# One more PSUM bank for a head's second level in the HGRN2 recurrence, and a new order on TensorE and VectorE at the change of heads

## The reference

```
bc = cumsum(log f)                                # within a chunk, per key feature
inter = einsum('bhtk,bhkv->bhtv', q * exp(b), state)
att   = einsum('bhtk,bhtsk,bhsk->bhts', q, exp(b_t - b_s), k)   # s <= t
o     = inter + einsum('bhts,bhsv->bhtv', att, v)
new_state = exp(b_last) * state + einsum('bhsk,bhsv->bhkv', k * exp(b_last - b), v)
```

## Time and profile before

| | us |
|---|---|
| median of 3 runs | 2068.59 |
| lowest and highest | 2065.93, 2070.22 |
| the profiled execution | 2072.03 |
| its span | 2070.4 |
| mean granted TensorE clock | 0.98 |
| TensorE busy | 1965.7 (95% of the span) |
| VectorE, ScalarE, GpSimd busy | 1573.7, 1342.5, 671.2 |
| the recurrence, from the first level's matmul (348.5 us) to the last output's (455.3 us) | about 107 |

### The profile page before, as it was taken

One profiled execution on the slowest core, in us unless ns is written; L12 is line 12 of the kernel. 1 busy time (PEld: TensorE's weight loads), 2 busy tenths in 40 slices (PEclk: granted clock), 3 DMA queues, 4 the chain that ended last, 5 costly groups with the idle time before them and its releaser, 6 DMA issues.

```text
span 2070.4 us, 39543 instructions
## 1 busy us (share of the span) xinstructions
PE 1965.7 (95%) x11106; PEld 1682.3 (81%) x11107; DVE 1573.7 (76%) x2202; ACT 1342.5 (65%) x1943; POOL 671.2 (32%) x758
## 2 busy tenths in 40 slices
PE   7999998879988999999999999999999999999995
PEld 6888877767776888889788897978897888979884
DVE  5334356865678788989888898889898888988886
ACT  5231156753436586877768677788777687777865
POOL 2200001321234242623425243344244252433423
PEclk9999999989978999999999999999999999999998
DMA  5322121113347898989899898999899998989987
GB/s 190 76 82 102 56 88 32 41 44 116 123 161 284 282 310 292 348 274 360 286 317 327 280 366 274 336 313 370 278 357 291 312 328 277 371 274 333 316 287 247
DMA packets 267759, 507.33 MB, mean 245 GB/s; under 512 B 39148, under 2 KB 44268, under 8 KB 267320
## 3 DMA queue, kind: packets, MB, share of 16 engines
q1 hardware_dynamic: 244042, 453.98, 63.8%
q0 software_dynamic: 23664, 52.67, 9.6%
HBM read 463.09 MB, written 43.53 MB: 245 GB/s over the span
## 4 chain that ended last, share of the span: by engine, by line
PE 64%; issue 1%; DMA 1%; POOL 1%; DVE 1%; ACT 0%; POOLq 0%; DVEq 0%; ACTq 0%
PE ps L1238 17%; PE ps L740 11%; PE ps L742 11%; PE ps L741 10%; PE ps L1240 7%; PE ps L1278 3%; PE ps L1279 3%; PE ps L1130 2%; PE ps L1211 1%; DMA raw<-acc_d,icur 0%; PE ps L1202 0%; DMA acc_d<-y,icur 0%; DVE wlo L2301 0%; ACT whi L1609 0%; DVE raw L2385 0%
## 5 line engine op out<-in xcount | busy, mean ns | idle before, releaser
L2301 DVE TENSOR_TENSOR wlo<-raw,whi 128x1024 fp32r<-128x1024 f32 x764 | 912.6, 1218 | 110.6 <-ACT whi L1609 90.0
L1609 ACT ACTIVATE whi<-raw 128x1024 fp32r<-128x1024 f32 x764 | 830.4, 1117 | 134.4 <-PE ps L1240 91.9
L1238 PE MATMUL ps<-xT,whi 128*128 128x320 f32 x1920 | 504.8, 349 | 6.2 <-issue 5.6
L1240 PE MATMUL ps<-xT,wlo 128*128 128x160 f32 x1920 | 456.1, 238 | 0.0
L1238 PEld LDWEIGHTS ps<-xT,whi 128*128 128x128 f32 x1920 | 363.3, 189 | 9.8 <-issue 6.0
L1240 PEld LDWEIGHTS ps<-xT,wlo 128*128 128x128 f32 x1920 | 369.3, 192 | 0.5
L2656 POOL DMA_INDIRECT acc_d<-y,icur x93 | 158.4, 1704 | 441.1 <-ACT y L1643 258.3
L740 PE MATMUL ps<-whi,xT 128*128 128x512 f32 x544 | 218.4, 401 | 3.3 <-DVE wlo L2157 3.3
L740 PE MATMUL ps<-whi,aT 128*128 128x512 f32 x512 | 212.9, 416 | 3.0 <-DVE aTl L2357 3.0
L742 PE MATMUL ps<-whi,xT 128*128 128x512 f32 x544 | 213.3, 392 | 0.0
L741 PE MATMUL ps<-wlo,xT 128*128 128x512 f32 x544 | 213.0, 391 | 0.0
(11 more groups left out here) (350 smaller groups left out, 3554.2 us busy)
## 6 DMA issues: line engine op xcount, KB each, us to landing
raw<-in_w SPq DMA_DIRECT2D x768, 512.0 KB
raw<-in_w_in SPq DMA_DIRECT2D x16, 512.0 KB
xs<-in_x SPq DMA_DIRECT2D x8, 512.0 KB, 8.8
raw<-in_w_out SPq DMA_DIRECT2D x8, 512.0 KB
mix<-in_x SPq DMA_DIRECT2D x8, 512.0 KB, 3.5
h_d<-h SPq DMA_DIRECT2D x8, 512.0 KB
acc_d<-mix SPq DMA_DIRECT2D x8, 512.0 KB
raw<-acc_d SPq DMA_DIRECT2D x8, 512.0 KB, 7.2
```

What stands on the lines that cost most here:

```text
L1238: pe.matmul(o2, wh[:, a, cols], xT2[:, :, k, 0:JOB_T], start=q == 0 and a == 0, stop=False, skip_group_check=True)
L1240: m = pe.matmul(o, wl[:, a, cols], xT2[:, 0, k, 0:JOB_T], start=False, stop=q == QUARTERS - 1 and a == 1, skip_group_check=True)
L1609: act.activation(parted(slot(whis, s)), paired(raw_slot(s), s), ACT.Copy).then_inc(split_hi, 1)
L2301: dve.tensor_tensor(parted(slot(wlos, s)), paired(raw_slot(s), s), parted(slot(whis, s).bitcast(F32)), ALU.subtract).then_inc(split_lo, 1)
```

## The change

Level 1 gets PSUM bank 1 instead of bank 2 (`ps[:, L]` where it was `ps[:, 2 * L]`). It no longer waits for the state chain, and on TensorE it goes ahead of the outputs of the head behind it. Level 2, which writes banks 0 and 1, waits for the copies of both levels 0 and 1. On VectorE the state chain moves from step 9h + 1 to step 9h + 2, behind `args` of level 2 and `prods` of level 1, and directly ahead of the diagonal. `used_by` follows the new order on TensorE. ScalarE's and GpSimd's orders are as before. Number, kind and size of all instructions are the same.

```diff
@@ used_by
-            if L == 0 and hd > 0:
+            if L < 2 and hd > 0:
                 return s
             if L == LEVELS + 1 and hd < HH - 1:
-                return s + 2
+                return s + 3
             return s + 1
@@ TensorE, level
                 elif L >= 2:
-                    pe.wait_ge(front_copied, 2 * hd + L - 1)
-                elif hd > 0 and L == 0:
+                    pe.wait_ge(front_copied, 2 * hd + 2)
+                elif hd > 0:
                     pe.wait_ge(level_copied, BACK * hd)
-                elif hd > 0:
-                    pe.wait_ge(states_set, hd)
...
-                        m = pe.matmul(ps[:, 2 * L, pair * P:(pair + 1) * P], keys_of, queries, start=True, stop=True)
+                        m = pe.matmul(ps[:, L, pair * P:(pair + 1) * P], keys_of, queries, start=True, stop=True)
@@ TensorE, the loop
             for hd in range(HH):
+                level(hd, 1)
                 if hd > 0:
                     outputs(hd - 1)
-                for L in range(1, LEVELS):
+                for L in range(2, LEVELS):
                     level(hd, L)
@@ ScalarE, front
-                                       ps[i:i + h, 2 * L, :].rearrange("p (t n) -> p t n", n=P)[:, :, i:i + h], ACT.Copy)
+                                       ps[i:i + h, L, :].rearrange("p (t n) -> p t n", n=P)[:, :, i:i + h], ACT.Copy)
@@ VectorE, the loop
-                if s >= 2:
+                if s >= 2 and (s == STEPS * HH + 1 or s % STEPS != 1):
+                    if s % STEPS == 2 and s > 2:
+                        copies(s - 3)
                     copies(s - 2)
```

## The result

The changed kernel takes 2082.34 us (median of 5 runs, 2077.70 to 2086.11) against 2068.59 (5 runs, 2065.93 to 2070.27): 13.75 us more. The ratio is 1.0070, with a 95% interval of 1.0059 to 1.0081.

A forecast was written before the change was run, and what follows sets the result against it. TensorE was taken to bound the kernel, with nothing to absorb the recurrence's losses. Three changes of heads 10.7, head 0 1.7 and the clock 3.6 sum to 16.0 us on 2068.59: 2084.6 us, range 2077 to 2090.

The forecast's parts named there:

- What bounds: Whole kernel: TensorE is busy 95% of the span, so what the recurrence loses or gains reaches the end in full.
- Level 1 ahead of the outputs: Change of heads on TensorE: level 1's 0.89 us of matmuls run under VectorE's state chain and cost nothing.
- The state chain's delay: VectorE at a change of heads: two operations put ahead of the chain make the outputs start 1.22 us late.
- Level 2's wait: TensorE behind the outputs: waiting for level 1's copies on ScalarE makes level 4 3.58 us late, 10.7 us in three changes.
- Head 0: First head: level 2 waits for the copies of level 1 and starts 1.7 us later, bounds 1.0 and 1.8.
- The clock: Levels 2 and 3: TensorE's clock falls to half behind each new idle stretch, 1.2 us each, 3.6 us in all.
- rival 1: Changes of heads: the clock stays up, so 12.4 us more, 2081.0 us; chance 0.25.
- rival 2: Levels 2 and 3: the clock stays low over both or longer, 19.3 us or more, 2087.9 to 2091 us; chance 0.11.
- Rival 3: Level 2's wait is harmless and only the states' delay counts: 3.7 us more, 2072.3 us; chance 0.04.
- Rival 4: Behind the outputs TensorE is what is late, so the change gains 5.9 us, 2062.7 us; chance 0.03.

The follow-up runs named there:

- kernel before with outs late: The kernel before with only outs moved on ScalarE behind the exponential of level 3 and the copies of level 1: 2066.79 us, ratio 0.9994 to 1.0012.
- second profile of the changed kernel: The changed kernel run again, unaltered, beside the others on one chip: 2085.68 us, +18.5 us against the kernel before.
- the filled one: The changed kernel with 12 unused identity matmuls behind the outputs of each head but the last: 2080.61 us, +13.4 us against the kernel before.
- banks-alone version: The kernel before with only level 1 in bank 1 and level 2 waiting for both fronts, orders on TensorE and VectorE unchanged: 2076.72 us, +9.0 us.

## Why the prediction was right

Step by step, with the size that each had.

- **What bounds.** What the recurrence loses reaches the end. The kernel before with outs late, whose recurrence is as long as before (92.3 us), had a profiled execution of 2067.54 us. Against that one the second profile of the changed kernel has 17.8 us more in the recurrence (110.1) and 18.1 more in all (2085.68); the filled one 13.2 and 13.8.
- **Level 1 ahead of the outputs** costs nothing: it runs under the state chain, as predicted, and GpSimd's two arguments beside that chain (2.72 us) left it at 2.27. In the row that the prediction took for this, 1.12 of GpSimd's 1.27 us lay inside the chain, not all of it.
- **The state chain's delay.** Predicted 1.22 us. From the masked copy of level 6 to the chain it is 7.50 us in head 1 (367.48 to 374.98) against 6.30 (367.43 to 373.73), but 7.86 in heads 2 and 3 against 6.37: 1.20, 1.49, 1.49. The extra 0.27 lies with the decayed queries (line 1976): 2.13 us instead of 1.22, of which `args` and `prods` behind them give back 0.64. GpSimd's argument of level 2 began 0.08 us ahead of them (427.14 and 427.22) and VectorE was held up; before it began 0.01 us ahead, and GpSimd was. The rows of the kernel before, and behind the cut GpSimd's in the changed one:

```profile
418.47 2.20 POOL L2551 TENSOR_TENSOR he<-hf,mix 128x512 f32<-128x512 f32 x1 [1.02 <-PE ps L964]
418.48 1.22 DVE L1977 TENSOR_TENSOR hpx<-hq,he 128x1024 f32<-128x1024 f32 x1
...
427.14 1.13 POOL L2552 TENSOR_TENSOR he<-hf,mix 128x512 f32<-128x512 f32 x1 [0.96 <-PE ps L962]
```

All profiles agree. In the changes from head 1 and from head 2 of the eight profiles with level 1 in bank 1, 16 in all, GpSimd began 0.06 to 0.09 us ahead and VectorE took 2.13 or 2.14 us; in the eight of the other four profiles GpSimd began 0.01 to 0.03 us ahead and VectorE took 1.22. The banks-alone version has the same 2.13 us and the same 0.3 us (27.14 against 26.85) with VectorE's old order, so it is not due to where the state chain stands. Why GpSimd comes earlier in these versions was not looked into.
- **Level 2's wait.** Predicted: an idle stretch of 3.35 us, 2.02 us for level 2, 2.75 us from its masked copy to level 4, +3.58 us a change. Measured: 3.35; 2.02 (442.65 to the copy at 444.71, less 0.04); 2.75; and 28.00 - 24.42 = 3.58 in head 1, 28.35 - 24.50 = 3.85 in head 3. The interval taken from head 0 for the collision with GpSimd was the right one.
- **Head 0.** Predicted +1.7; 20.54 against 18.91, +1.63. In the banks-alone version it is +1.5, in the other three profiles with this wait +1.9, the clock being at half for 6.8 us instead of 3.4.
- **The clock.** Predicted: a fall at each change for 1.2 us. The size was nearly right (1.2 to 1.9 each), the frequency was not: 1 of 3 in one profile, 3 of 3 in another. The reason given for it, that the stretch is longer than that of head 0, does not hold up, since two of three such stretches in the first profile left the clock up, and shorter ones brought it down. Two falls fewer than forecast are 2.4 us, which is the gap between 16.0 us forecast and 13.75 measured the first time. Between the two profiles of the changed kernel the recurrence differs by 3.6 us, most of the 4.7 between 13.75 and the 18.5 of the second set; the rest is open. The clock goes with the spread of the changed kernel's runs too, 8.4 us in the first set against 4.3 for the kernel before: from the fastest to the slowest of the five, 2077.70 to 2086.11 us, the mean granted clock was 0.983, 0.982, 0.981, 0.980 and 0.978.
- **The rivals.** The forecast's chain of waits held. How near its number came is in part luck: 2082.34 lies nearer to rival 1's 2081.0 than to the forecast's 2084.6, and the second set, at +18.5, nearer to rival 2's +19.3 than to the forecast's +16.0. Rival 1 (a clock that stays up, 12.4 us) describes the filled kernel, at 13.4, and two of the three heads of the first profile. Rival 3 (3.7 us) would have needed level 2's wait to be harmless, and the banks-alone version's +9.0 refutes it. Rival 4 named what decides, ScalarE's order; changing that order in fact gives back about 9 us, but the kernel stays 4.3 us slower than the one before, and with level 2 freed as well it only comes level. The 5.9 us of gain appeared nowhere.

What stays open: why the clock falls at one passage of the same idle stretch and not at the next, and behind two short stretches as well. No run was made to vary where the stretch lies in time alone.

## What to carry to other kernels

Moving work ahead on one engine helps only if every engine that consumes it takes it early too: here level 1's product was complete 4.5 us sooner in a head's period (9.2 instead of 13.6 us behind the last masked copy), and its copies on ScalarE ended 1.5 us later (17.4 instead of 15.9), because they kept their place behind a copy that waits for the very step that had been moved back. When a change makes a wait cover more (here two fronts instead of one), read who is queued in front of the thing waited for, and who stands behind the waiting instruction on its own engine. And when a critical engine is given an idle stretch of two or three microseconds, count the clock as a second price, and a wider spread of the runs with it.

## What the runs showed of the hardware that was not expected

- Useless matmuls in an idle stretch are worth 5.1 us in three heads (2085.68 to 2080.61): with them the granted clock was 1.00 (2.4 GHz) in the level behind, without them 0.50 to 0.54 (1.2 GHz). In the kernel before, nine in each of three places brought only 1.7 us.
- Whether a stretch of 3.35 us brings the clock down differs from one head to the next (1 of 3 in one profile) and from one execution to the next of the same program (3 of 3 in the other). One profile is not enough to say that it does or does not.
- VectorE's operations with two SBUF operands took about twice as long under GpSimd's (0.69 to 1.66, 1.22 to 2.13 us), and which of the two engines was held up went with whether GpSimd began 0.01 to 0.03 or 0.06 to 0.09 us ahead. In these runs that added 0.3 us in two of the three changes of heads, at a place that the edits do not touch.
